# Seven more key blocks fetched ahead of the decode attention, and page transfers that wait for ten transposed blocks

## What is computed

```python
h = layer_norm(ALPHA * x + 0.5 * swiglu(x, ffn1_wi, ffn1_wo))
qa, ka, va, qb, kb, vb, qi, ki, wi = h @ w_in
# decode, mixer A: keys and values of the window buffer, cache_a_kv (8, 2048, 2, 12, 64)
for window, dil in ((128, 1), (512, 4), (2048, 16)):
    logits = einsum('bthd,btjhd->bthj', q, k_all[:, idx]) + bias
    o, lse = softmax(logits) @ v_all[:, idx], ...
# decode, mixer B: cache_b (160 pages, 128 rows, k 64 | v 64 | indexer key 64)
score = sum_h(relu(qi @ ki_all) * wi);  idx = top_k(score, 256)
o_b = softmax(qb @ k[idx] + bias) @ v[idx]
x = layer_norm(ALPHA * h + concat(o_a, o_b) @ w_out);  x = layer_norm(ALPHA * x + 0.5 * swiglu(x, ...))
```

## Time and profile before

| | |
|---|---|
| time, median of 3 runs | 1505.06 us (1504.9 to 1505.38) |
| profiled execution: its time, its span | 1506.47 us, 1504.8 us |
| busy share of the span: PE, weight loads, DVE, ACT, POOL | 93%, 85%, 37%, 30%, 39% |
| key stage, in the profile | 759.5 to 872.9 us |
| value stage, in the profile | 875.3 to 945.6 us |

### The profile page before, as it was taken

One profiled execution on the slowest core, in us unless ns is written; L12 is line 12 of the kernel. 1 busy time (PEld: TensorE's weight loads), 2 busy tenths in 40 slices (PEclk: granted clock), 3 DMA queues, 4 the chain that ended last, 5 costly groups with the idle time before them and its releaser, 6 DMA issues.

```text
span 1504.8 us, 30727 instructions
## 1 busy us (share of the span) xinstructions
PE 1398.4 (93%) x12059; PEld 1281.2 (85%) x12059; DVE 551.6 (37%) x1340; ACT 451.7 (30%) x833; POOL 593.0 (39%) x367
## 2 busy tenths in 40 slices
PE   6999999999988899997877898889999999999988
PEld 6999999999978777975555566878999999999988
DVE  5222222210251237667889723154222222201354
ACT  2122222211251233246644531135222222211441
POOL 6334433455553212221446102545334333454542
PEclk9999999999999999999999999898999999999999
DMA  6399665866243522432189889343655657755221
GB/s 225 98 268 317 235 221 179 282 215 221 88 152 120 170 70 78 158 110 61 30 232 281 259 294 312 127 163 119 212 197 197 213 181 255 255 192 199 71 68 46
DMA packets 102942, 269.83 MB, mean 179 GB/s; under 512 B 44497, under 2 KB 44882, under 8 KB 102328
## 3 DMA queue, kind: packets, MB, share of 16 engines
q1 hardware_dynamic: 98216, 257.44, 51.4%
q0 software_dynamic: 3584, 8.39, 1.9%
q10 hardware_dynamic: 1040, 2.62, 1.1%
HBM read 259.78 MB, written 109.10 MB: 245 GB/s over the span
## 4 chain that ended last, share of the span: by engine, by line
PE 77%; DVE 7%; POOL 3%; ACT 3%; DMA 3%; issue 3%; SPq 3%; ACTq 0%; DVEq 0%; POOLq 0%
PE bank L1567 21%; PE bank L1571 20%; PE bank L1569 20%; DMA cache_a_ring<-in_cache_a 2%; POOL w_rest L543 2%; DVE idx_scores L1409 2%; PE bank L2095 2%; PE bank L1912 1%; PE bank L1800 1%; PE bank L1924 1%; PE bank L1902 1%; PE bank L1615 1%; SPq L433 1%; SPq L435 1%; DMA w_raw<-in_w_w_in 1%
## 5 line engine op out<-in xcount | busy, mean ns | idle before, releaser
L543 POOL TENSOR_TENSOR w_rest<-w_raw,w_high 128x1024 fp32r<-128x1024 f32 (+2 forms) x162 | 417.7, 2578 | 659.4 <-ACT w_high L708 659.4
L1567 PE MATMUL bank<-x_high,w_high 128*128 128x272 f32 x1856 | 394.6, 294 | 19.9 <-POOL x_rest L553 11.4
L708 ACT ACTIVATE w_high<-w_raw 128x1024 fp32r<-128x1024 f32 (+2 forms) x162 | 183.6, 1134 | 750.6 <-PE bank L1571 680.1
L1571 PE MATMUL bank<-x_high,w_rest 128*128 128x272 f32 x1856 | 385.1, 289 | 0.0
L1569 PE MATMUL bank<-x_rest,w_high 128*128 128x272 f32 x1856 | 384.2, 289 | 0.0
L1567 PEld LDWEIGHTS bank<-x_high,w_high 128*128 128x128 f32 x1856 | 291.5, 189 | 40.8 <-issue 35.5
L1569 PEld LDWEIGHTS bank<-x_rest,w_high 128*128 128x128 f32 x1856 | 293.1, 189 | 0.0
L1571 PEld LDWEIGHTS bank<-x_high,w_rest 128*128 128x128 f32 x1856 | 291.2, 190 | 0.0
L1010 DVE SCALAR_TENSOR_TENSOR hidden<-silu_gate,bank 128x272 f32<-128x272 f32 x88 | 34.6, 434 | 392.6 <-ACT silu_gate L726 392.6
L1567 PE MATMUL bank<-hidden_high,w_high 128*128 128x272 f32 x616 | 127.7, 288 | 0.0
L1571 PE MATMUL bank<-hidden_high,w_rest 128*128 128x272 f32 x616 | 127.5, 288 | 0.0
(11 more groups left out here) (302 smaller groups left out, 1802.4 us busy)
## 6 DMA issues: line engine op xcount, KB each, us to landing
out_a_sample<-in_cache_a SPq DMA_DIRECT2D x73, 1344.0 KB
w_raw<-in_w_wi SPq DMA_DIRECT2D x88, 512.0 KB, 5.2
cache_a_ring<-in_cache_a SPq DMA_DIRECT2D x112, 384.0 KB, 4.9
w_raw<-in_w_wo SPq DMA_DIRECT2D x32, 704.0 KB, 5.3
w_raw<-in_w_w_in SPq DMA_DIRECT2D x26, 512.0 KB, 3.7
w_raw<-in_w_gate SPq DMA_DIRECT2D x8, 640.0 KB, 3.9
idx_pages_ring<-in_cache_b SPq DMA_DIRECT2D x128, 32.0 KB, 1.8
bias_toeplitz<-rev_bias POOLq DMA_DIRECT2D x32, 128.0 KB, 2.7
```

The costliest lines, as they stand in the source:

```text
L543: nc.gpsimd.tensor_tensor(WL[:, s, 0:tiles, :], RAW[:, slot, 0:tiles, :], WH[:, s, 0:tiles, :].bitcast(F32), ALU.subtract).then_inc(S["lo_ ...
L708: nc.scalar.activation(WH[:, s, 0:tiles, :], RAW[:, slot, 0:tiles, :], ACT.Copy).then_inc(S["hi_ready"], 1)
L1567: mm(banks[n][:, 0:HALF], wh, xh[n], start=start, stop=False)
L1571: last = mm(banks[n][:, 0:HALF], wl, xh[n], start=False, stop=stop)
```

## The change

- Ten key blocks are now asked for before the end of the prompt attention instead of three: blocks 0 to 2 in ring slots as before, and seven extra ones, 3 to 9, in a place of their own: three over chunks 0 to 4 of PROJ, four over its chunks 12 to 17, which nobody reads any more. Each has a semaphore of its own.
- The other 49 blocks take turns in the five ring slots: blocks 10 and 11 are issued where 3 and 4 were, and block 12, 13, 14, 15 wait for the transpose of block 0, 1, 2, 10; from there on, block n waits for block n - 5 again.
- The extra blocks lie where KVP's pages will land. So POOL waits for ten transposed blocks ahead of its first page, and SP issues its first page behind block 15. SP's 64 pages are then spread five for three keys and end with block 52.
- The order of the value slots is turned by one, to follow the slots that come free.

```diff
@@ -68,7 +68,10 @@
 CHUNK_AT = (0, 64, 32, 96)
 PAIRS = DEC_BATCH // 2
 KEY_RING, VALUE_RING = 5, 7
-VALUE_SLOTS = (1, 2, 3, 4, 0, 5, 6)
+VALUE_SLOTS = (4, 0, 1, 2, 3, 5, 6)
+EARLY_RING, EARLY_EXTRA = 3, 7
+EARLY = EARLY_RING + EARLY_EXTRA
+N_RING = 56 - EARLY_EXTRA
 N_VALUE_STEPS = 32
 B_PROBS_FROM, B_VALUES_FROM, B_OUT_STEP = 19, 24, 28
 KEYS_A = 128 * KEY_BLOCKS_A
@@ -226,6 +229,8 @@
 
         AR = sb("cache_a_ring", [128, VALUE_RING, WIDTH_A], at=split_at)
         KTA = sb("k_a_t", [128, 2, WIDTH_A], at=split_at + KEY_RING * WIDTH_A * 4)
+        KX_LOW = sb("k_a_early_low", [128, 3, WIDTH_A], at=h_at)
+        KX_HIGH = sb("k_a_early_high", [128, 4, WIDTH_A], at=h_at + C_VA * T * 4)
         KTB = sb("k_b_t", [128, 2, 512], at=e_at + 2208)
         assert split_at + VALUE_RING * WIDTH_A * 4 <= h_at
 
@@ -276,6 +281,7 @@
         S = {n: ctx.enter_context(nc.semaphore(n)) for n in names}
         raw_loaded = [ctx.enter_context(nc.semaphore(f"raw_loaded{i}")) for i in range(RAW_SLOTS)]
         toe_in = [ctx.enter_context(nc.semaphore(f"toe_in{i}")) for i in range(4)]
+        early_in = [ctx.enter_context(nc.semaphore(f"early_in{i}")) for i in range(EARLY_EXTRA)]
         ar_in = [ctx.enter_context(nc.semaphore(f"ar_in{i}")) for i in range(VALUE_RING)]
         pg_in = [ctx.enter_context(nc.semaphore(f"pg_in{i}")) for i in range(4)]
         kv_in = [ctx.enter_context(nc.semaphore(f"kv_in{i}")) for i in range(8)]
@@ -359,10 +365,31 @@
 
             return n + 1 + n // 14
 
-        KEY_LOADS = [len(range(slot, 56, KEY_RING)) if slot < KEY_RING else 0 for slot in range(VALUE_RING)]
+        KEY_LOADS = [len(range(slot, N_RING, KEY_RING)) if slot < KEY_RING else 0 for slot in range(VALUE_RING)]
+
+        def key_turn(n):
+
+            return n if n < EARLY_RING else n - EARLY_EXTRA
+
+        def key_of_turn(r):
+
+            return r if r < EARLY_RING else r + EARLY_EXTRA
+
+        def is_extra(n):
+
+            return EARLY_RING <= n < EARLY
+
+        def key_block(n):
+
+            if not is_extra(n):
+                return AR[:, key_turn(n) % KEY_RING, :]
+            e = n - EARLY_RING
+            return KX_LOW[:, e, :] if e < 3 else KX_HIGH[:, e - 3, :]
 
         def key_landed(n):
-            return ar_in[n % KEY_RING], 16 * (n // KEY_RING + 1)
+            if is_extra(n):
+                return early_in[n - EARLY_RING], 16
+            return ar_in[key_turn(n) % KEY_RING], 16 * (key_turn(n) // KEY_RING + 1)
 
         def value_slot(m):
             return VALUE_SLOTS[m % VALUE_RING]
@@ -473,37 +500,44 @@
                 return cache_a[b, r0:r0 + 128, cols]
 
             def load_keys(n):
-                if n >= KEY_RING:
-                    sp.wait_ge(S["ka_t"], n - KEY_RING + 1)
-                sp.dma_start(AR[:, n % KEY_RING, :], cache_rows(n, 0)).then_inc(ar_in[n % KEY_RING], 16)
+                if n >= EARLY and key_turn(n) >= KEY_RING:
+                    sp.wait_ge(S["ka_t"], key_of_turn(key_turn(n) - KEY_RING) + 1)
+                landed, _ = key_landed(n)
+                sp.dma_start(key_block(n), cache_rows(n, 0)).then_inc(landed, 16)
 
             def load_values(m):
                 slot = value_slot(m)
                 if m >= VALUE_RING:
                     sp.wait_ge(S["va_used"], (m - VALUE_RING) // 2 + 1)
                 elif slot < KEY_RING:
-                    sp.wait_ge(S["ka_t"], 56 - (55 - slot) % KEY_RING)
+                    sp.wait_ge(S["ka_t"], key_of_turn(N_RING - 1 - (N_RING - 1 - slot) % KEY_RING) + 1)
                 else:
                     sp.wait_ge(S["ka_sc"], scores_done(54 + slot - KEY_RING))
                 sp.dma_start(AR[:, slot, :], cache_rows(m, 1)).then_inc(ar_in[slot], 16)
 
-            for n in range(3):
+            for n in range(EARLY_RING):
+                load_keys(n)
+            sp.wait_ge(S["ix_relu"], 3 * IDX_HEADS)
+            sp.wait_ge(S["qblocks_done"], 1)
+            for n in range(EARLY_RING, EARLY_RING + 3):
                 load_keys(n)
             sp.wait_ge(S["lo_ready"], FIRST["w_out"])
             sp.dma_start(OHB[:], onehots[:, KEY_BLOCKS_A:24, :]).then_inc(S["oh_in"], 16)
             sp.dma_start(TOPC[:], consts[:, 356:740]).then_inc(S["topc_in"], 16)
+            sp.wait_ge(S["proj_out"], 48)
+            for n in range(EARLY_RING + 3, EARLY):
+                load_keys(n)
             sp.wait_ge(S["pt_ps"], 2 * N_STEPS)
-            for n in range(3, KEY_RING):
+            for n in range(EARLY, EARLY + KEY_RING - EARLY_RING):
                 load_keys(n)
-            sp.wait_ge(S["proj_out"], 48)
             sp.wait_ge(S["new_rows_out"], 16 * 2 * DEC_BATCH)
             sp.wait_ge(S["o_sb"], 8)
             sp.dma_start(VN2[:], a_sample[:, PAST - DEC_SEQ:PAST, WIDTH_A:2 * WIDTH_A]).then_inc(S["vnew_in"], 16)
 
             page_at = 0
-            for n in range(KEY_RING, 56):
+            for n in range(EARLY + KEY_RING - EARLY_RING, 56):
                 load_keys(n)
-                while page_at < min(64, (5 * (n - 4) + 3) // 4):
+                while n > EARLY + 4 and page_at < min(64, (5 * (n - EARLY - 4) + 2) // 3):
                     load_kv_page(sp, 2 * page_at)
                     page_at += 1
             for m in range(56):
@@ -668,6 +702,7 @@
             pool.wait_ge(S["ids_in"], 16)
             pool.wait_ge(S["proj_out"], 48)
             pool.wait_ge(S["o_sb"], 8)
+            pool.wait_ge(S["ka_t"], EARLY)
             for q in range(1, DEC_BATCH * PAGES, 2):
                 load_kv_page(pool, q)
 
@@ -1967,7 +2002,7 @@
                         pe.wait_ge(S["ka_sb"], n - 1)
                     for c in range(6):
                         last = tr(BANK[2 * (n % 2) + c // 4][:, 128 * (c % 4):128 * (c % 4) + 128],
-                                  AR[:, n % KEY_RING, 128 * c:128 * c + 128], IDENT)
+                                  key_block(n)[:, 128 * c:128 * c + 128], IDENT)
                     last.then_inc(S["ka_t"], 1)
                 if n >= 1:
                     key_scores_a(n - 1)
```

## The result

The changed kernel took 1515.05 us (median of 5 runs, 1511.91 to 1517.98) against 1505.06 us (5 runs, 1500.87 to 1513.41): a ratio of 1.0063, 95% interval 1.0037 to 1.0089, so +9.5 us with +5.6 to +13.4 around it. It is slower. The profiled execution took 1512.29 us with a span of 1510.6 us, 5.8 more than before's span.

The account below looks back on a forecast made before the run. The prediction took SP's stream of load issues to bound the key stage, with the DMA engines close behind. It added +8.0 us for the later last key issue and -0.2 after it to 1505.06, giving 1512.9 us, range 1507 to 1516.

Parts of the forecast that it names:

- SP's stream bounds the key stage: Key stage, the forecast itself: SP's unpaused issuing of loads sets the time, giving 1512.9 us; chance 0.72.
- The price of an issue: SP, block 15 to 55: about 1.14 us a page, 0.50 a plain key block; 94.8 us, plus 3.5 of pauses.
- The hole: Early key stage: SP rests from about 763.3 to 773.8 us, 10.5 us, until block 10 is transposed.
- Block 55 8.0 us later: End of SP's key loads: block 55 issued at 872.1 instead of 864.13 us, +8.0 us (+4.5 to +9.0).
- The tail, -0.2 us: From block 55's issue to the value stage: +0.3 us for bunched last blocks, -0.5 for quicker landing.
- The early loads cost nothing: Prompt attention, about 670 to 690 us: seven key blocks moved there cost 0 us.
- the cover: Prompt attention: third head pair's bias, first used at 685.10 us, lands by 685.4 at most; failure costs one or two us.
- POOL and the value stage: POOL's pages run from 772.4 to near 848 us, read at 873.9; value stage unchanged, 0 us (-1 to +1).
- The sum, +7.8: Whole kernel: +8.0 us for the later block 55 and -0.2 after it, bounds +2.5 to +11.0 us.
- The rival of the transfers: Key stage: the DMA engines bound it, so the change adds only 0.8 us, 1505.9 us; chance 0.13.
- The faster rival: Key stage: SP's rest costs nothing, seven issues and small waits go, -7.7 us, 1497.4 us; chance 0.05.

## Why the prediction was right

The forecast was slower, 1512.9 us within 1507 to 1516; it came out at 1515.05.

- *SP's stream bounds the key stage.* Right, and shown by taking 16 pages from it (-10.1 us in the stage with the same transfers).
- *The price of an issue.* From block 15 to block 55 the sum was 94.8 us and 3.5 of pauses, 98.3. It took 97.9, with 4.3 us of waits, so 93.6 for the rest. That the sum is off by only 0.4 us is in part luck: two errors of about 1 us had opposite signs.
- *The hole.* Block 15 was to go out at 773.8, 14.3 us after the stage's start. Its issue ended at 773.6 in a stage that started 0.8 us sooner. SP's rest was to be 10.5 us, and its longest wait was 10.4.
- *Block 55 8.0 us later.* From the stage's start it was 104.6 us before and 112.2 in the changed kernel: +7.6.
- *The tail, -0.2 us.* From block 55's issue to the first value product it took 11.2 us before and 10.3 after: -0.9. Most of the difference was chance: before, the last transposes took 1.54 us, at a granted clock of 0.50, and 0.88 us after, at 1.00. This is the term whose size was off, by 0.7 us.
- *The early loads cost nothing.* The worst case that was to show the cover, 685.4 (676.3 + 9.0 is 685.3), lies behind the first use at 685.10, so it proved nothing. No cost was shown: bias tables landed within 9.4 us at most, DVE didn't wait for them, and the loads alone gave a ratio of 1.0001. But the prompt attention was 2 us longer on average in the profiles with early loads, which single profiles neither show to be a cost nor rule out. One of the two tables behind them is wanted earlier than the prediction says: DVE asks for it when it merges the lists, at 824.0 us before. It had landed long before.
- *POOL and the value stage.* POOL's pages ran from 773.3 to 848.4 us and were first read at 879.7; the value stage kept its 74.6 us. The instructions on mixer B's pages in the changed kernel, columns as in the earlier trace rows:

```profile
L360 POOL DMA_DIRECT2D kv_b_pages<-in_cache_b x64: 722/722/746, 773.3 to 848.4; - x64
...
L2019 PE MATMUL bank<-consts_sb,kv_b_pages x64: 272/273/331, 879.7 to 915.1; 128*128 128x128 f32 x64
```

- *The sum, +7.8.* The stage grew by 6.7 in the profile, the median by 9.5 with 5.6 to 13.4; both fit. The runs of one kernel scatter by several us, so the total alone could not have told 6.7 from 7.8. Of the chances, 0.14 for no change and 0.06 for faster don't follow quite from the cases (0.13 + 0.02 and 0.05); the forecast doesn't hang on it.

The rival of the transfers falls: the DMA engines were busy for 85% after the hole, and the moved pages changed the stage at equal bytes. It held some truth as the next bound: in the kernel before with POOL's 80 pages and earlier logits they were 101% busy. For the key blocks the statement of the Trainium skill (DMA: Bandwidth & Descriptors, Issuing engines are not separate DMA queues) that issue time is "usually small relative to the DMA itself" agrees with the trace: 0.50 us of issue against an estimated 1.16 us of the DMA engines' time. For pages whose number is read first, 1.14 us each on SP against an estimated 0.30, it doesn't, and moving 16 of them to a second issuing engine took 10.1 us off.

The faster rival needed block 10 through PE by 766 us; it was through at 773.0. But that a version without the hole beats before is true: the one with free pages first and an even pace has a stage 3.5 us shorter, though its ratio of 0.9985 (0.9968 to 1.0002) doesn't show it clearly in the total.

## What to carry to other kernels

Before moving transfers ahead, count the issues of the queue that makes them and not only the bytes: a wait put ahead of a queue's work costs its full length when that queue never rests (here 10.4 us, of which the seven issues made ahead of it gave some 3.6 back). When a buffer is reused, order the later tenants so that those beside the early ones go first; here that gave back 10 us, together with an even pace of the pages. And when one bound is taken away, read the chain again: SP's issues, DVE's order and the DMA engines stood within some us of each other, so each change alone gained little and all together 18 us (12 of them without the early blocks).

## What the hardware showed unexpectedly

The DMA engines' busy share doesn't measure what is left in them. Before, they were 94% busy at 274 GB/s; in the kernel with POOL's 80 pages and earlier logits they moved 318 GB/s at 101%:

```profile
773.00:858.80 85.80, 69.85 (x952) 50.33 (x955) 78.58 (x218) 44.22 (x101) 49.71 (x69) 0.98 1.01 318
```

In this stretch 50 blocks and 110 pages were issued. By the estimates of 1.16 and 0.30 us, worked out from busy shares, they are 91.0 us of DMA work; the engines were busy for 86.7. So these two prices don't carry over from one stretch to another. This goes the same way as the stage of 100.5 us where 104 to 108 were expected, but it isn't shown to be the only reason. Why the busy time is less for about the same transfers was not tried.
